# Attention output of a hybrid decoder step: queries on partitions, divided after the product, in place of probabilities scaled before it

## The chip, the cores and the metric

The kernel runs on one core of one Trainium2 chip. The metric is the device time of one execution in microseconds (us); three runs of the kernel before took 1811.17, 1813.03 and 1814.5 us, so its median is 1813.03 us. Besides these there is one profiled execution, from which all rows below come.

## The reference, cut to what matters

The program is one inference step of a two-layer decoder trunk for 512 prompt tokens and 64 sample tokens. Each layer projects its input, runs sparse attention and a gated linear recurrence (GLA) beside each other, merges both with gates, and ends in a SwiGLU block. The change is in the attention of the prompt tokens: 8 heads of 64, 4 key/value heads, and each query keeps its best 128 keys.

```python
logits = jnp.einsum('bqhgd,bqkhd->bqhgk', qg, k_sel) * HEAD_DIM ** -0.5
logits = jnp.where(valid[:, :, None, None, :], logits, -jnp.inf)
p = jax.nn.softmax(logits, axis=-1)
o = jnp.einsum('bqhgk,bqkhd->bqhgd', p, v_sel)
...
merged = sigmoid(gate_a) * (attn_o @ w_oa) + sigmoid(gate_b) * (g_out @ w_ob)
```

The kernel computes logits against all keys up to the query and masks those that are not kept, so that nothing is gathered.

## The kernel before, in words

All activations stand turned, features on partitions and the 576 tokens along the free axis, in two halves of 288. Weights are read panel by panel; a panel is 128 output features. Each is split into a high and a low part (w_hi by ScalarE in line 1996, w_lo by GpSimd in line 1895), and a panel is worked off in eight parts of six matmuls (line 1460): high by high, high by low, low by high, each for two halves.

The class Plan writes out one list of steps; every engine walks through this list and issues what is its own, so the order on each engine's queue is the list's order. Where smaller work lies beside the panels, the method woven spreads the parts of the panels over a list of items: each item has a weight (FILL, 1.0 where it names none), and after an item come as many parts as its weight's share of all the parts. The stretch of the change holds the last 80 parts of the gate panels (gr, gta, gtb) against the items of the GLA's norm, the sample group's attention, and then the prompt's attention.

The prompt's attention goes through four blocks j of 128 queries, and in each through 8 heads h; block j has j+1 blocks of 128 keys. Head number n = 8j+h takes this way. PE computes its logits (lines 1475 and 1476) while head n-2 is handled. The vector engine masks them in place and takes the maximum (max_head, line 2408). ScalarE writes the exponentials to p_t, of which there are two, and their sum to p_sum (line 2005). The vector engine takes the reciprocal of the sum and multiplies p_t by it (scale_head, lines 2417 and 2419); in the queue of the vector engine the scaling of head n+1 stands ahead of the maximum of head n+2. PE turns p_t block by block by transposes into PSUM bank 2 (line 1859), and ScalarE copies that to pT_t (line 2335). After every second head the step attn_pv multiplies for both heads of one key/value head (line 1871): V's 128x64 slice is the stationary operand, the turned probabilities of 128 queries stream, and the result has features on partitions, the even head on the lower 64 and the odd head on the upper. The four products of a block fill PSUM bank 3, the use ("o", j). After the last one the step attn_t has ScalarE copy the bank to attn_t (line 2342).

Behind the stretch stands the step mix: ScalarE splits gla_o and then attn_t into in_hi (lines 2264 and 2269), the vector engine makes in_lo (line 2373), and PE starts the output panels (oab). It can start once the last gtb panel is done, because in_hi is the input of the gtb panels up to then. SP loads the first weights of the SwiGLU block when ("o", 3) is ready.

Other names in the rows: soT (line 1845) turns the sample group's output, four PE instructions with 128x128 weights and 64 streamed columns; k_t,qz (line 1811) are logits of the sample group; gate_b (line 2462) is the vector engine's eviction of a gate panel out of PSUM; q_split and k_hi (line 2323) are ScalarE's splits of the next block's queries and keys.

Of the kernel before, what the change touches and what calls it, by code (L numbers as in the profile page):

```python
# [17 lines left out]
F32 = mybir.dt.float32  # L18
# [9 lines left out]
P = 128  # L28
# [14 lines left out]
HD = 64  # L43
# [40 lines left out]

FILL = {"intra": 2.0, "intra_out": 1.5, "kv": 1.0, "sround": 2.0, "attn": 1.0, "attn_pv": 0.4, "attn_t": 0.2,
        "topk": 0.5, "kcT": 1.0, "slog": 2.4, "gnorm": 2.0}
# [158 lines left out]
class Plan:  # L245
# [220 lines left out]
    def build_layer(self, base):  # L466
# [81 lines left out]
        for j, h in order:  # L548
            items.append([("attn", j, h)])
            if h < 5 and j < 3:  # L550
                items[-1] += [("qk", j + 1, i) for i in ((0, 1), (2,), (3,), (4,), (5,))[h]]
            if h % 2:
                items.append([("attn_pv", j, h // 2)])
            if h == N_HEADS - 1:
                items[-1].append(("attn_t", j))
        self.woven(range(split, first["oab"]), items)
# [59 lines left out]
    def extra_step(self, step):  # L616
# [61 lines left out]
        if kind == "attn_pv" and step[2] == 0:  # L678
            self.open(("o", step[1]), 3)
        if kind == "gnorm":  # L680
            self.open(("gn", step[1], 0), 0)
            self.open(("gn", step[1], 1), 1)
            self.stage(("gn", step[1]), "bank_ready", ("gn", step[1], 1))
            self.gate_tmp(("gn", step[1]), "gnorm_done", self.layer * GH + step[1] + 1)
# [3 lines left out]
def build(nc, A):  # L688
# [4 lines left out]
    with ctx:  # L693
# [124 lines left out]
        pT_t = sub("pT_t", [P, 2, 4, P])  # L818
        o_pairs = at("o_pairs", [P, 2, KV_W], F32, off[0])
        sub("o_pairs_kept", [P, ATTN_W])  # L820
        cursor[0] = max(off[0], end1, ar + 2 * turned + 2 * FF_SLOTS * 4 * P * 4)
# [107 lines left out]
        pv_done = semaphore("pv_done")  # L929
        p_scaled = semaphore("p_scaled")  # L930
        p_inverted = semaphore("p_inverted")
# [429 lines left out]
        def _(e):  # L1361
# [24 lines left out]
            def body():  # L1386
# [133 lines left out]
                for layer, step in plan.steps:  # L1520
# [329 lines left out]
                    elif kind == "attn":  # L1850
                        _, j, h = step
                        n = j * N_HEADS + h
                        if n == 0:
                            logits(0)
                            logits(1)
                        e.wait_ge(p_scaled, nth(n + 1, len(ORDER)))
                        e.wait_ge(free(("pT", j, h)), opened(("pT", j, h)))
# [5 lines left out]
                    elif kind == "attn_pv":  # L1863
                        _, j, kv = step
                        if kv == 0:
                            e.wait_ge(free(("o", j)), opened(("o", j)))
                        for u in range(2):
                            e.wait_ge(free(("pT", j, 2 * kv + u)), emptied(("pT", j, 2 * kv + u)))
                        for s in range(j + 1):
                            for u in range(2):  # L1870
                                ins = e.matmul(aux[64 * u:64 * u + 64, 3, kv * P:(kv + 1) * P],  # L1871
                                               kv_rows[:, s, KV_W + kv * HD:KV_W + (kv + 1) * HD], pT_t[:, u, s, :],
                                               start=(s == 0), stop=(s == j), skip_group_check=True)
                        if kv < N_KV - 1:
                            ins.then_inc(pv_done, 1)
                        else:
                            ins.then_inc(ready(("o", j)), 1)

            body()
# [90 lines left out]
        def _(e):  # L1970
# [18 lines left out]
            def body():  # L1989
# [30 lines left out]
                for layer, step in plan.steps:  # L2020
# [237 lines left out]
                    elif kind == "mix":  # L2258
# [6 lines left out]
                        else:  # L2265
                            e.wait_ge(free(("so",)), emptied(("so",)))
                            e.wait_ge(free(("o", 3)), emptied(("o", 3)))
                            for kt in range(4, KD):
# [70 lines left out]
                    elif kind == "attn_t":  # L2339
                        j = step[1]  # L2340
                        e.wait_ge(ready(("o", j)), filled(("o", j)))
                        e.activation(attn_t[:, :, j * P:(j + 1) * P], aux[:, 3, :].rearrange("p (m n) -> p m n", m=4),
                                     ACT.Copy).then_inc(free(("o", j)), 1)

# [4 lines left out]
        def _(e):  # L2349
# [18 lines left out]
            def body():  # L2368
# [31 lines left out]
                def max_head(n):  # L2400
# [9 lines left out]
                    e.wait_ge(max_done, turn(max_done))  # L2410

                def scale_head(n):

                    j, h = ORDER[n]
                    key = ("log", j, h)
                    e.wait_ge(free(key), emptied(key))
                    e.reciprocal(p_inv[:, h:h + 1], p_sum[:, j % 2, h:h + 1]).then_inc(dve_step, 1)
                    e.wait_ge(dve_step, turn(dve_step))
                    e.tensor_scalar(p_t[:, n % 2, 0:(j + 1) * P], p_t[:, n % 2, 0:(j + 1) * P], p_inv[:, h:h + 1], None,
                                    ALU.mult).then_inc(p_scaled, 1)  # L2420

                for layer, step in plan.steps:
# [473 lines left out]
                    elif kind == "spT":  # L2896
                        i = step[1]
                        if i >= 2:
# [6 lines left out]
                                      aux[0:NS, 2, 2 * P:3 * P]).then_inc(free(("spT", i)), 1)  # L2905
                        e.wait_ge(free(("spT", i)), emptied(("spT", i)))
                    elif kind == "attn":
                        _, j, h = step
                        n = j * N_HEADS + h
                        L = (j + 1) * P  # L2910
                        if n == 0:
                            max_head(0)
                            max_head(1)
                            scale_head(0)
                        if n + 1 < len(ORDER):
                            scale_head(n + 1)
                        if n + 2 < len(ORDER):
# [35 lines left out]
```

## Time and profile before

| what | value |
|---|---|
| runs | 1811.17, 1813.03, 1814.5 us (median 1813.03) |
| profiled execution | 1812.7 us, of which the span is 1810.9 us |
| mean granted TensorE clock | 0.992 |
| busy | PE 1743.2 us (96%), PE weight load 1634.2 (90%), vector engine 1092.6 (60%), ScalarE 795.9 (44%), GpSimd 784.1 (43%) |
| DMA | 151.06 MB, mean 83 GB/s |

The span goes from the first to the last instruction; the 1.8 us around it belong to the execution's time. PE's busy time is the time in which a matmul is under way; matmuls are pipelined, so records overlap and a busy PE need not be at its peak. The chain of waits is followed back from the last instruction, at each step to what released it. In a timeline a row stands for one or several instructions of one kind in a row: start, length from the first start to the last end, engine, line, operands, count, and in brackets how long the engine idled before and what ended that.

### The profile page before, as it was taken

To read this page: it belongs to the slowest core of one execution; us is meant where nothing else is said; L and a number is where in the kernel's file an instruction comes from. 1 tells how busy PE (TensorE), PEld (TensorE's weight loads), DVE (VectorE), ACT (ScalarE), POOL (GpSimd) and SP (SyncE) were. 2 spreads that over 40 slices of the span, in tenths; PEclk is the share of its full clock that TensorE was granted. 3 is DMA by queue.
4 is the path that set the end of the run, shared out by engine and by line. 5 is a ranking of instruction groups with operands and counts; after the bars stand their busy time and mean duration, and the time that the engine had idled before them with its cause. 6 is when DMAs were issued, how large, how long until landed. Compare 5 with 4: busy or idle time off the path is not lost.

```text
span 1810.9 us, 33288 instructions
## 1 busy us (share of the span) xinstructions
PE 1743.2 (96%) x12738; PEld 1634.2 (90%) x12738; DVE 1092.6 (60%) x2142; ACT 795.9 (44%) x1539; POOL 784.1 (43%) x510
## 2 busy tenths in 40 slices
PE   8999999999999999999999899999999999999998
PEld 6885898789999999999988768987899999999998
DVE  3856776455587437537537567845647873574463
ACT  4442214564466336426434322236645662463352
POOL 2323451533446447446333323525234563563452
PEclk9999999999999999999999999999999999999999
DMA  4232234214323423413222222351233233234122
GB/s 156 69 86 70 61 89 124 59 36 129 93 59 94 119 68 94 116 43 88 62 74 74 62 74 74 80 143 40 78 94 105 56 97 109 67 94 114 50 57 79
DMA packets 263303, 151.06 MB, mean 83 GB/s; under 512 B 15910, under 2 KB 255594, under 8 KB 263146
## 3 DMA queue, kind: packets, MB, share of 16 engines
q1 hardware_dynamic: 263146, 148.94, 29.3%
q8 instruction: 102, 1.67, 0.4%
q14 instruction: 55, 0.45, 0.1%
HBM read 141.53 MB, written 7.37 MB: 82 GB/s over the span
## 4 chain that ended last, share of the span: by engine, by line
PE 79%; DVE 13%; ACT 4%; issue 3%; DMA 1%; SPq 0%; POOL 0%; DVEq 0%; ACTq 0%; POOLq 0%
PE prod L1460 36%; PE prod L1514 8%; PE prod L1515 8%; PE prod L1516 8%; PE prod L1404 2%; PE prod L1405 2%; PE prod L1406 2%; PE aux L1871 1%; PE aux L1859 1%; DVE in_lo L2373 1%; PE aux L1834 1%; DVE aux L2619 1%; DVE scores L2788 1%; PE aux L1632 1%; ACT w_hi L1996 1%
## 5 line engine op out<-in xcount | busy, mean ns | idle before, releaser
L1895 POOL TENSOR_TENSOR w_lo<-w_raw,w_hi 128x1024 fp32r<-128x1024 f32 (+2 forms) x160 | 370.3, 2314 | 735.2 <-ACT w_hi L1996 730.7
L1996 ACT ACTIVATE w_hi<-w_raw 128x1024 fp32r<-128x1024 f32 (+2 forms) x160 | 163.0, 1019 | 269.4 <-PE prod L1460 236.3
L1460 PE MATMUL prod<-in_hi,w_hi 128*128 128x288 f32 x1024 | 236.7, 313 | 10.2 <-DVE in_lo L2373 7.8
L1460 PE MATMUL prod<-in_hi,w_lo 128*128 128x288 f32 x1024 | 223.0, 300 | 0.0
L1460 PE MATMUL prod<-in_lo,w_hi 128*128 128x288 f32 x1024 | 222.7, 300 | 0.0
L1514 PE MATMUL prod<-t_hi,ff_hi 128*128 128x288 f32 x704 | 208.6, 296 | 1.2 <-ACT in_sum L2050 0.6
L1460 PE MATMUL prod<-mid_hi,w_hi 128*128 128x288 f32 x960 | 207.6, 298 | 2.1 <-DVE mid_lo L2373 2.1
L1515 PE MATMUL prod<-t_lo,ff_hi 128*128 128x288 f32 x704 | 207.9, 295 | 0.0
L1516 PE MATMUL prod<-t_hi,ff_lo 128*128 128x288 f32 x704 | 207.1, 294 | 0.0
L1460 PE MATMUL prod<-mid_lo,w_hi 128*128 128x288 f32 x960 | 206.3, 296 | 0.0
L1460 PE MATMUL prod<-mid_hi,w_lo 128*128 128x288 f32 x960 | 206.3, 296 | 0.0
L1460 PEld LDWEIGHTS prod<-in_hi,w_hi 128*128 128x128 f32 x1024 | 167.5, 193 | 27.2 <-issue 19.1
L1460 PEld LDWEIGHTS prod<-in_hi,w_lo 128*128 128x128 f32 x1024 | 168.5, 193 | 0.0
L1460 PEld LDWEIGHTS prod<-in_lo,w_hi 128*128 128x128 f32 x1024 | 168.1, 193 | 0.0
L1907 POOL TENSOR_TENSOR ff_lo<-ff_sum,ff_hi 128x512 fp32r<-128x512 f32 x88 | 126.9, 1445 | 81.7 <-ACT ff_hi L2046 81.3
L1460 PEld LDWEIGHTS prod<-mid_hi,w_hi 128*128 128x128 f32 x960 | 153.6, 188 | 3.5 <-DVE mid_lo L2373 3.5
L1514 PE MATMUL prod<-in_hi,ff_hi 128*128 128x288 f32 x528 | 156.3, 296 | 0.4 <-issue 0.4
L1515 PE MATMUL prod<-in_lo,ff_hi 128*128 128x288 f32 x528 | 155.8, 295 | 0.0
L1516 PE MATMUL prod<-in_hi,ff_lo 128*128 128x288 f32 x528 | 155.6, 295 | 0.0
L1460 PEld LDWEIGHTS prod<-mid_hi,w_lo 128*128 128x128 f32 x960 | 154.0, 188 | 0.0
L1460 PEld LDWEIGHTS prod<-mid_lo,w_hi 128*128 128x128 f32 x960 | 153.9, 188 | 0.0
L1514 PEld LDWEIGHTS prod<-t_hi,ff_hi 128*128 128x128 f32 x704 | 132.1, 188 | 2.9 <-issue 1.8
(332 smaller groups left out, 3688.1 us busy)
## 6 DMA issues: line engine op xcount, KB each, us to landing
w_raw<-in_w_in SPq DMA_DIRECT2D x72, 512.0 KB, 3.7
ff_gate<-in_w_ffn_gu SPq DMA_DIRECT2D x44, 512.0 KB, 5.0
ff_up<-in_w_ffn_gu SPq DMA_DIRECT2D x44, 512.0 KB, 3.9
w_raw<-in_w_ffn_down SPq DMA_DIRECT2D x32, 512.0 KB, 3.8
w_raw<-in_w_o SPq DMA_DIRECT2D x16, 512.0 KB, 3.7
w_raw<-in_w_ffn_down SPq DMA_DIRECT2D x16, 384.0 KB, 3.3
k_pages<-in_cache_k SPq DMA_DIRECT2D x32, 128.0 KB, 2.1
v_pages<-in_cache_v SPq DMA_DIRECT2D x32, 128.0 KB, 2.1
```

The lines of the kernel that those rows point to most:

```text
L1404: e.matmul(out, in_hi[:, kt, tok], hi_w, start=first, stop=False)
L1405: e.matmul(out, in_hi[:, kt, tok], lo_w, start=False, stop=False)
L1406: ins = e.matmul(out, in_lo[:, kt, tok], hi_w, start=False, stop=last)
L1460: ins = e.matmul(slot(g)[:, h, :], w[:, slot_w, i * P:(i + 1) * P], a[:, i, h * HALF:(h + 1) * HALF], start=first, stop=last)
L1514: e.matmul(out, ff_hi[:, q % FF_SLOTS, w], hi, start=first, stop=False, skip_group_check=True)
L1515: e.matmul(out, ff_hi[:, q % FF_SLOTS, w], lo, start=False, stop=False, skip_group_check=True)
L1516: ins = e.matmul(out, ff_lo[:, q % FF_SLOTS, w], hi, start=False, stop=(k == 3), skip_group_check=True)
L1632: ins = e.matmul(aux[:, bank(key), 0:L], qi_t[rows, h // 2, j * P:(j + 1) * P], ki_t[rows, 0:L], start=True, stop=True)
L1834: ins = e.matmul(aux[64 * u:64 * u + 64, bank(("spo", i)), 0:KV_W], pT_t[0:n, i % 2, s, 64 * u:64 * u + 64], v, start=(s == 0), stop=(s == 2),
L1895: e.tensor_tensor(w_lo[:, p % 2, 0:n], w_raw[:, p % RAW_RING, 0:n], w_hi[:, p % 2, 0:n].bitcast(F32), ALU.subtract).then_inc(w_lo_done, 1)
L1907: e.tensor_tensor(ff_lo[:, q % FF_SLOTS, :], ff_weights(name, b), ff_hi[:, q % FF_SLOTS, :].bitcast(F32), ALU.subtract).then_inc(ff_lo_don ...
L1996: e.activation(w_hi[:, p % 2, 0:n], w_raw[:, p % RAW_RING, 0:n], ACT.Copy).then_inc(w_hi_done, 1)
```

## The change

The exponentials are no longer scaled. The transposes of a head wait for its exponential itself. In attn_pv the operands change places: the turned exponentials of 128 queries are the stationary operand (128x128) and a 128x64 slice of V streams, so the result has queries on partitions and the 8 heads' 64 features each along the free axis of bank 3. A new step attn_norm on the vector engine takes the reciprocals of the block's eight sums at once and multiplies the bank by them into o_rows. A new step attn_t on PE turns o_rows by four transposes back into bank 3, a use of its own, ("ot", j), and ScalarE copies that as before. The weaving gets items for these: attn_norm with weight 0.2 after the last product of a block, the turning with the next block's first head, and at the end an empty item and the turning of block 3, each at 1.0.

```diff
-FILL = {... "attn_pv": 0.4, "attn_t": 0.2,
+FILL = {... "attn_pv": 0.4, "attn_norm": 0.2,
...
                 items.append([("attn_pv", j, h // 2)])
+            if h == 0 and j:
+                items[-1].append(("attn_t", j - 1))
             if h == N_HEADS - 1:
-                items[-1].append(("attn_t", j))
+                items.append([("attn_norm", j)])
+        items += [[], [("attn_t", 3)]]
...
+        if kind == "attn_t":
+            self.open(("ot", step[1]), 3)
...
+        o_rows = at("o_rows", [P, N_HEADS, HD], F32, off[0])
...
# PE, attn
-                        e.wait_ge(p_scaled, nth(n + 1, len(ORDER)))
+                        e.wait_ge(free(("log", j, h)), emptied(("log", j, h)))
...
# PE, attn_pv
-                        for s in range(j + 1):
-                            for u in range(2):
-                                ins = e.matmul(aux[64 * u:64 * u + 64, 3, kv * P:(kv + 1) * P],
-                                               kv_rows[:, s, KV_W + kv * HD:KV_W + (kv + 1) * HD], pT_t[:, u, s, :],
+                        for u in range(2):
+                            for s in range(j + 1):
+                                h = 2 * kv + u
+                                ins = e.matmul(aux[:, 3, h * HD:(h + 1) * HD], pT_t[:, u, s, :],
+                                               kv_rows[:, s, KV_W + kv * HD:KV_W + (kv + 1) * HD],
                                                start=(s == 0), stop=(s == j), skip_group_check=True)
...
+                    elif kind == "attn_t":
+                        j = step[1]
+                        e.wait_ge(free(("o", j)), emptied(("o", j)))
+                        for m in range(4):
+                            ins = e.transpose(aux[:, 3, m * P:(m + 1) * P],
+                                              o_rows[:, 2 * m:2 * m + 2, :].rearrange("p h d -> p (h d)"), ident)
+                        ins.then_inc(ready(("ot", j)), 1)
...
# ScalarE, mix and attn_t
-                            e.wait_ge(free(("o", 3)), emptied(("o", 3)))
+                            e.wait_ge(free(("ot", 3)), emptied(("ot", 3)))
...
-                        e.wait_ge(ready(("o", j)), filled(("o", j)))
+                        e.wait_ge(ready(("ot", j)), filled(("ot", j)))
...
# vector engine
-                def scale_head(n):
-
-                    j, h = ORDER[n]
-                    key = ("log", j, h)
-                    e.wait_ge(free(key), emptied(key))
-                    e.reciprocal(p_inv[:, h:h + 1], p_sum[:, j % 2, h:h + 1]).then_inc(dve_step, 1)
-                    e.wait_ge(dve_step, turn(dve_step))
-                    e.tensor_scalar(p_t[:, n % 2, 0:(j + 1) * P], p_t[:, n % 2, 0:(j + 1) * P], p_inv[:, h:h + 1], None,
-                                    ALU.mult).then_inc(p_scaled, 1)
...
+                    elif kind == "attn_norm":
+                        j = step[1]
+                        e.wait_ge(free(("log", j, N_HEADS - 1)), emptied(("log", j, N_HEADS - 1)))
+                        e.reciprocal(p_inv[:], p_sum[:, j % 2, :]).then_inc(sums_inverted, 1)
+                        e.wait_ge(sums_inverted, nth(j + 1, 4))
+                        e.wait_ge(ready(("o", j)), filled(("o", j)))
+                        e.tensor_tensor(o_rows[:], aux[:, 3, :].rearrange("p (h d) -> p h d", d=HD),
+                                        bcast(p_inv[:], 2, HD), ALU.mult).then_inc(free(("o", j)), 1)
+                        e.wait_ge(free(("o", j)), emptied(("o", j)))
...
-                            scale_head(0)
-                        if n + 1 < len(ORDER):
-                            scale_head(n + 1)
```

## Rows read from the trace of the kernel before

**Rows 1.** The page, part 4: the chain that ended last, by engine.

```profile
PE 79%; DVE 13%; ACT 4%; issue 3%; DMA 1%; SPq 0%; POOL 0%; DVEq 0%; ACTq 0%; POOLq 0%
```

**Rows 2.** Windows: length, busy time (instructions) by engine, clock, DMA share, GB/s.

```profile
331.24:411.02 79.78, 72.54 (x582) 65.19 (x581) 44.07 (x136) 49.01 (x131) 31.10 (x25) 0.98 0.13 37
...
334.70:338.10 3.40, 3.40 (x17) 3.38 (x16) 1.82 (x8) 2.32 (x8) 2.00 (x2) 0.50 0.54 154
1229.00:1232.40 3.40, 3.40 (x17) 3.38 (x15) 1.25 (x6) 2.13 (x8) 2.38 (x3) 0.50 0.51 148
```

**Rows 3.** Waits of PE, whole span: us in total, times, longest.

```profile
PE prod L1460 <- DVE in_lo L2373: 7.8, 4, 2.2
...
PE aux L1871 <- ACT pT_t L2335: 5.3, 10, 1.2
...
PE aux L1859 <- DVE p_t L2419: 3.9, 4, 1.8
```

**Rows 4.** Timeline of PE, a product of block 0 and one of block 3.

```profile
350.16 0.43 PE L1460 MATMUL prod<-in_hi,w_lo 128*128 128x288 f32 x2
350.53 0.44 PE L1871 MATMUL aux<-pT_t,kv_rows 128*64 128x128 f32 x4
350.89 0.53 PE L1460 MATMUL prod<-in_hi,w_hi 128*128 128x288 f32 x2
...
397.44 0.43 PE L1460 MATMUL prod<-in_hi,w_lo 128*128 128x288 f32 x2
397.80 1.09 PE L1871 MATMUL aux<-pT_t,kv_rows 128*64 128x128 f32 x16
398.83 0.66 PE L1859 MATMUL aux<-cst,p_t 128*128 128x128 f32 x4
```

**Rows 5.** Timeline of PE, a head of block 3.

```profile
396.02 0.60 PE L1859 MATMUL aux<-cst,p_t 128*128 128x128 f32 x4
396.37 0.47 PE L1475 MATMUL aux<-k_hi,q_split 128*128 128x512 f32 x1
...
396.91 0.43 PE L1460 MATMUL prod<-in_hi,w_hi 128*128 128x288 f32 x2
```

**Rows 6.** Timeline of PE around soT.

```profile
329.74 0.42 PE L1460 MATMUL prod<-in_hi,w_lo 128*128 128x288 f32 x2
330.00 0.55 PE L1845 MATMUL aux<-cst,o_pairs 128*128 128x64 f32 x4
330.37 0.51 PE L1460 MATMUL prod<-in_hi,w_hi 128*128 128x288 f32 x2
```

**Rows 7.** Timeline of PE, logits of the sample group.

```profile
300.28 0.40 PE L1811 MATMUL aux<-k_t,qz 128*64 128x64 f32 x8
```

**Rows 8.** Groups by line, vector engine: busy, mean ns; idle before, releaser.

```profile
L2462 DVE TENSOR_TENSOR gate_b<-prod,rstd 128x576 f32<-128x576 f32 x16 | 12.1, 758 | 12.9 <-PE prod L1460 12.6
```

**Rows 9.** Timelines of ScalarE and PE at the first head.

```profile
332.72 0.19 ACT L2005 ACTIVATION_READ_ACCUMULATOR p_t<-aux,neg_max 128x1 f32 x1
...
333.98 0.33 PE L1859 MATMUL aux<-cst,p_t 128*128 128x128 f32 x1 [1.78 <-DVE p_t L2419]
```

**Rows 10.** Timeline of ScalarE at the start of block 1.

```profile
351.70 0.59 ACT L2342 ACTIVATE attn_t<-aux 128x512 f32<-128x512 f32 x1
...
353.43 0.62 ACT L2323 ACTIVATE q_split<-q_t 64x512 fp32r<-64x512 f32 x1
...
354.26 0.36 ACT L2335 ACTIVATE pT_t<-aux 128x256 f32<-128x256 f32 x1
```

**Rows 11.** Groups by line, PE's weight loads: busy, mean ns; idle before, releasers.

```profile
L1859 PEld LDWEIGHTS aux<-cst,p_t 128*128 128x128 f32 x160 | 19.3, 140 | 8.4 <-DVE p_t L2419 4.7 <-issue 3.8
L1871 PEld LDWEIGHTS aux<-pT_t,kv_rows 128*64 128x64 f32 x320 | 17.3, 136 | 11.6 <-ACT pT_t L2335 7.9 <-issue 3.7
```

**Rows 12.** Timelines of ScalarE and PE at the stretch's end.

```profile
409.41 2.39 ACT L2264 ACTIVATE in_hi<-gla_o 128x576 fp32r<-128x576 f32 x4
...
411.02 0.50 PE L1460 MATMUL prod<-in_hi,w_hi 128*128 128x288 f32 x2 [2.15 <-DVE in_lo L2373]
```

More of the change, by code:

```diff
@@ L83 @@
 Y_STORES = {3: 0, 6: 4, 7: 7}
-FILL = {"intra": 2.0, "intra_out": 1.5, "kv": 1.0, "sround": 2.0, "attn": 1.0, "attn_pv": 0.4, "attn_t": 0.2,
+FILL = {"intra": 2.0, "intra_out": 1.5, "kv": 1.0, "sround": 2.0, "attn": 1.0, "attn_pv": 0.4, "attn_norm": 0.2,
         "topk": 0.5, "kcT": 1.0, "slog": 2.4, "gnorm": 2.0}
@@ L929, in build @@
         pv_done = semaphore("pv_done")
-        p_scaled = semaphore("p_scaled")
+        sums_inverted = semaphore("sums_inverted")
         p_inverted = semaphore("p_inverted")
@@ L2340, in body @@
                         j = step[1]
-                        e.wait_ge(ready(("o", j)), filled(("o", j)))
+                        e.wait_ge(ready(("ot", j)), filled(("ot", j)))
                         e.activation(attn_t[:, :, j * P:(j + 1) * P], aux[:, 3, :].rearrange("p (m n) -> p m n", m=4),
-                                     ACT.Copy).then_inc(free(("o", j)), 1)
+                                     ACT.Copy).then_inc(free(("ot", j)), 1)
             body()
```

## The prediction

> **What bounds the kernel now.** I read the page's chain of waits first: TensorE (PE) is 79% of what ended last and the vector engine 13% [rows 1], so a change pays only where it alters PE's own instructions or a wait of PE. The view by windows narrows it to the stretch that the change touches: 79.78 us in the first layer, PE busy in 72.54, mean granted clock 0.98; behind the 0.98 stands one piece of 3.4 us at 0.50, which is 1.2 of 2.4 GHz, and a like piece in the second layer [rows 2]. The table of PE's waits names what stands in that stretch over both layers: 5.3 us for pT_t, 3.9 us for the scaled p_t, and half of the 7.8 us for in_lo, at the stretch's end [rows 3]. Last comes the timeline of PE, for the price of each group of instructions.
>
> I count per layer; both run the same plan. A panel's part is three pairs of matmuls; a pair begins 0.265 us after the one before (it is 0.43 long, and the next overlaps it). A group's price is the gap before it beyond that step, its run to the next start, and what the instruction behind it is longer than usual.
>
> **The second product (attn_pv).** The number of matmuls stays: 8(j+1) in block j, two PE instructions each, so 16 groups per layer of 4, 8, 12 or 16 instructions, four of each. Now 64 columns of V are the weights and 128 columns stream. A group of 4: from 350.16+0.265 to 350.53 a gap of 0.10, 0.36 to the next start, and the pair behind is 0.53 long for 0.43: 0.56 us. A group of 16: gap 0.095, 1.03 to the next start, and the transposes behind are 0.66 long where other fours are 0.60: 1.19 us [rows 4, 5]. In a line between them: 0.56, 0.77, 0.98, 1.19; four of each are 14.0 us.
> Afterwards the weights are 128 columns (a turned block of exponentials) and 64 stream. One group of before has that shape in both operands, soT: its four instructions begin without a gap, take 0.37 to the next start, and the pair behind is 0.51 long for 0.43: 0.45 us, 0.11 an instruction [rows 6]. In proportion: 0.44, 0.88, 1.32, 1.76; four of each are 17.6 us. So **+3.6 us**: short groups get cheaper, long ones dearer. Bounds: without what follows the group, 0.37/4 = 0.093 a step, 2.7 us less; on the other side transposes of 0.60/4 = 0.15, their first one's start included, 6 us more. Further off lies k_t,qz (64 columns as weights, 64 streamed): eight in 0.40, 0.05 each at most [rows 7]; by it the groups come to 8 us, 6 less than before. I stay with soT, which is alike in both operands.
> The Trainium skill (TensorE: Matmul & The Clock Gate, section Back-to-back issue gap) gives streamed columns / 2.4 GHz + 2.5 ns for a back-to-back matmul, 29 ns here; by it the groups would come to some 5 us. soT speaks against it for full weights, and the same section warns that weight load and matmul both set the pace.
>
> **The new transposes (attn_t on PE).** Four 128x128 transposes per block, 16 per layer. A group of four takes 0.35 to the next start [rows 5]; with 0.08 behind it, as after soT, 0.43: **+1.7 us** (bounds 1.4 and, at its full length of 0.60, 2.4).
> The Trainium skill (TensorE: Matmul & The Clock Gate, Part 4: PE-mode transpose) gives about 275 ns for a transpose within a kernel. Four in a row cost 0.35 in the trace; by the page's figure the sum would be some 2.7 us more per layer.
>
> **The division (attn_norm).** Per block one reciprocal of 128x8 and one product of 128x512 out of PSUM; the nearest row is gate_b, 0.76 at 576 columns [rows 8], so 0.7, and about 0.95 with drain and signals from the last product's end to the first turning transpose (bounds 0.7 and 1.3). What lies beside it follows from the weaving: the items' weights rise from 67.0 to 69.8 (four norms of 0.2, an empty item and attn_t at 1.0), the parts per unit fall from 80/67 = 1.194 to 1.146. A head's transposes and logits take 0.89 for four key blocks, so 0.22 a block [rows 5]; a part takes 3 x 0.265 = 0.8. Rounded out, behind block 0's last product come a part and a head of two blocks (1.24), covered; behind block 1's only a head of three (0.67), short by 0.3; behind block 2's a head of four, short by 0.1; behind block 3's two parts, covered. **+0.4 us.** Behind the waiting product on the vector engine stands the next block's third maximum, whose logits PE issues about when the product ends: nothing.
>
> **The removed scaling.** 32 reciprocals and 32 products per layer leave the vector engine, which is not the bound. PE sees:
> (a) the start. The first exponential's sum is out at 332.72+0.19 = 332.91, PE starts at 333.98 after 1.78 idle [rows 9]; released by ScalarE it starts about 0.1 behind the sum: **-0.96**.
> (b) the clock. Right behind that gap PE runs 3.4 us at 0.50, in both layers [rows 2]. With a gap of about 0.9 I expect full speed, worth half the piece: **-1.7** (bounds 0 and -1.7).
> (c) one further wait for a scaling, 3.9/2-1.78: **-0.2** [rows 3].
> (d) the waits for pT_t, 2.65. The loop of exponential, reciprocal, scaling, next maximum, next exponential is cut, since no maximum stands behind a scaling any more. Not all goes: at block 1's first product ScalarE works off q_split to pT_t from 353.43 to 354.62, and the copy attn_t (0.59), which stood ahead of that head's exponentials, moves in between [rows 10]. I count 0.6 of wait there and 1.1 in small ones elsewhere: **-0.95** (bounds +0.5, where two more copies show, and -2.65).
> (e) gaps ahead of weight loads that the profile puts down to issue, 3.8 and 3.7 in both layers [rows 11]; most of that lies under a matmul still running. I give **-0.5** (0 to -1.9).
>
> **The end of the stretch.** The last parts of gtb now follow the turning, and the split of gla_o starts only behind them. Before, PE idled 2.15 after the last product; from the split's start to PE's next matmul are 411.02-409.41 = 1.61 [rows 12], with a signal 1.7: **-0.4** (0 to -0.5). Block 3's copy is hidden under the last part; if it were not, it costs its 0.6. SP's loads of ff_gate still wait for the last product, and the weights' steps on ScalarE and POOL keep their panels: nothing.
>
> **Sum** per layer: 3.6+1.7+0.4-0.96-1.7-0.2-0.95-0.5-0.4 = +1.0; two layers **+2.0 us**. The profiled execution has a span of 1810.9 and a time of 1812.7, so it would take 1814.7; it lies 0.3 below the median of the runs, 1813.0, to which +2.0 gives **1815.0**.
>
> **Rivals.**
> 1. The clock still falls (slower). One mechanism at one place: PE's gap at the first head, then about 0.9 us and among short transposes and logits, still brings 0.50 behind it. Price 2 x 1.7: 1818.4. For it: it fell in both layers. Against: the 0.98 over the whole stretch leaves room for one such piece only, so none followed the 1.2 us wait for pT_t [rows 2, 3]. It decides from one layer on: 1816.7 with one.
> 2. All waits go (faster). With the loop cut, (d) and (e) empty to their bounds: 2 x (1.7+1.4) = 6.2 more, 1808.8. For it: each maximum stood behind an exponential. Against: ScalarE's own queue, with the copy moved into it.
> 3. Streamed columns set the product's price (the rule above): at 0.05 a step 2 x 9.6 less, 1795.8. Only k_t,qz speaks for it, and its weights are half as wide.
> 4. The turning does not fit its cover (slower): the o bank is held by product, division, turning and copy, and a block's first product waits for the copy. If that costs 0.7, a copy and its signal, at three blocks of both layers: +4.2, 1819.2. ScalarE has 49 of 79.78 us to do [rows 2], so I think it rare.
>
> **How the numbers follow.** Forecast 0.47; rival 1 0.2, rival 4 0.1, rival 2 0.19, rival 3 0.04. About 0.2% (3.6 us) is what a measurement of this kernel tells from no change, so 1809.4 to 1816.6 is the same. The forecast's own spread is some +-4 (the product's step, (d)), which lends a little to both sides: faster 0.25, same 0.43, slower 0.32. Range 1807.5 to 1820.5: from a little below rival 2 to a little above rivals 1 and 4; left out are rival 3 and cases in which two costs add.
>
> **What would show it.** The product's group of 16 takes about 1.76 us and begins without a gap, the group of 4 gets shorter. The turning transposes take 0.35 and wait at most 0.3 for o_rows. PE's gap before the first transposes is near 0.9, and the window behind it shows clock 1.00. The waits for pT_t fall from 5.3 to some 3.5, the largest at block 1's first product. The gap before the output panels is near 1.7. I am wrong if the product's step is not near 0.11, if the clock stays at 0.50 there, or if PE waits more for pT_t than before.

## The result: slower, 1832.2 us for the 1815.0 predicted

The changed kernel took 1832.2 us (median of 4 runs, 1827.5 to 1835.8), the kernel before 1813.0 beside it: ratio 1.0104, 95% interval [1.0083, 1.0125]. Timed once more among the experiments, it took 1825.5 us (6 runs) beside 1814.1, ratio 1.0074 [1.0056, 1.0092]. So it is slower by 19 us in the one and by 11 us in the other; the prediction had +2.0 and a range that ended at +7.5. What differs between the two timings is in part 6 of the experiments.

Its chain of waits reads as before, TensorE (PE) first [rows 1]:

```profile
PE 80%; DVE 12%; ACT 4%; issue 2%; DMA 1%; SPq 0%; POOL 0%; DVEq 0%; ACTq 0%; POOLq 0%
```

The stretch of [rows 2], from the sample group's last product to the output panels, and the two pieces right behind the first head (columns: length, busy us and instructions of PE, PEld, DVE, ACT, POOL, granted clock, DMA share, GB/s):

```profile
335.58:421.73 86.15, 80.29 (x604) 76.49 (x603) 26.57 (x80) 50.76 (x132) 30.76 (x25) 0.98 0.15 42
338.10:341.50 3.40, 3.40 (x17) 3.38 (x17) 0.72 (x4) 2.27 (x9) 3.07 (x3) 0.51 0.12 15
1239.30:1242.70 3.40, 3.40 (x16) 3.38 (x16) 0.72 (x4) 2.43 (x9) 3.18 (x3) 0.50 0.18 32
```

The vector engine has lost 17.5 of its 44.1 us. PE is busy 7.8 us longer, of which 0.8 is a part that the new weaving moved into the stretch. Behind the first head the clock is still at 0.50 in both layers.

PE's waits over the whole span (total us, times, longest), to be laid beside [rows 3]:

```profile
PE prod L1466 <- DVE in_lo L2387: 6.8, 4, 1.7
PE aux L1878 <- ACT pT_t L2349: 4.5, 10, 0.7
...
PE aux L1865 <- ACT p_t L2019: 2.8, 2, 1.4
```

So 1.0, 0.8 and 1.1 us of waiting have gone, over both layers. The rest of the answer is in PE's own instructions. Timelines of PE: a product of block 3, to be laid beside [rows 4], then block 0's turning and the stretch's end, beside [rows 12]:

```profile
397.57 0.43 PE L1466 MATMUL prod<-in_hi,w_lo 128*128 128x288 f32 x2
397.84 1.89 PE L1878 MATMUL aux<-kv_rows,pT_t 128*128 128x64 f32 x16
399.57 0.60 PE L1865 MATMUL aux<-cst,p_t 128*128 128x128 f32 x4
...
353.47 0.60 PE L1889 MATMUL aux<-cst,o_rows 128*128 128x128 f32 x4
353.83 0.52 PE L1466 MATMUL prod<-in_hi,w_hi 128*128 128x288 f32 x2
...
421.73 0.50 PE L1466 MATMUL prod<-in_hi,w_hi 128*128 128x288 f32 x2 [1.68 <-DVE in_lo L2387]
```

The group of 16 begins one step (0.27) behind the pair ahead of it, without a gap, and takes 1.73 to the next start, where it took 1.03. This turning takes 0.36 and waits for nothing.

**Where the start's gain went.** Timelines of ScalarE, the vector engine, POOL and PE at the first head, layer 1:

```profile
334.93 1.35 ACT L2319 ACTIVATE attn_t<-aux 64x64 f32<-64x64 f32 x8 [1.62 <-PE aux L1851]
336.30 1.06 ACT L2010 ACTIVATE w_hi<-w_raw 128x1024 fp32r<-128x1024 f32 x1
337.38 0.37 ACT L2019 ACTIVATE p_t<-aux,neg_max 128x128 f32<-128x128 f32 x1
...
336.54 0.14 DVE L2422 DVE_READ_ACCUMULATOR2_ANT neg_max<- 128x1 f32 x1
...
337.89 0.33 PE L1865 MATMUL aux<-cst,p_t 128*128 128x128 f32 x1 [1.38 <-ACT p_t L2019]
```

The masked maximum is ready at 336.68, but ScalarE starts the exponential at 337.38: a panel's w_hi stands ahead of it. Before, that panel's start lay one item earlier (w_hi at 329.66). The items' new weights moved it, as they move every part.

### The profile page after: what moved, and what is told of

It is laid out like the page before. It is cut to its first block, busy times and chain, and to the rows that moved or that the text cites. A ratio compares the mean times of both kernels' runs of the same rounds, so it can differ in the third digit from the quotient of the medians.

```text
span 1830.2 us, 33256 instructions
## 1 busy us (share of the span) xinstructions
PE 1762.6 (96%) x12770; PEld 1659.8 (91%) x12770; DVE 1058.6 (58%) x2030; ACT 798.1 (44%) x1539; POOL 784.0 (43%) x510
## 4 chain that ended last, share of the span: by engine, by line
PE 80%; DVE 12%; ACT 4%; issue 2%; DMA 1%; SPq 0%; POOL 0%; DVEq 0%; ACTq 0%; POOLq 0%
PE prod L1466 36%; PE prod L1520 8%; PE prod L1521 8%; PE prod L1522 8%; PE prod L1410 2%; PE aux L1878 2%; PE prod L1411 2%; PE prod L1412 2%; PE aux L1865 1%; PE aux L1840 1%; DVE aux L2623 1%; DVE scores L2792 1%; PE aux L1638 1%; DMA x_rows<-in_x_prompt 1%; DVE mid_lo L2387 1%
```

## The experiments

Times are medians; a ratio is to the kernel before on the same chip. "At full clock" means a length less half of what of it lay at 0.50. The attention region is that of the last 80 input parts ahead of the output panels of a layer.

**1. The scaling alone (e1), the product alone (e2), the weaving alone (e3), and the change without its weaving (e4).**

e1 takes the scaling out of the kernel before and puts nothing in its place:

```
-                            scale_head(0)
-                        if n + 1 < len(ORDER):
-                            scale_head(n + 1)
```

> The kernel before with the scaling of the exponentials left out (its attention output is therefore not divided by the sums); products, weaving and layouts as before. Theory 1 (the price of the product's instructions and of the turning makes the loss, and the removed scaling gives little): the first transposes start about 1 us earlier per layer, one wait of 0.2 goes, the waits for pT_t shrink by less than half; 1 to 4 us less than before, 1809 to 1812; more only if the halved clock behind the first head goes (3.4 less). Rival (the freed vector engine is worth much, and the changed product takes it back): 6 us less or more.

Measured: 1809.6 us, ratio 0.9979 [0.9967, 0.9991]. Theory 1 holds: some 4 us are all that the removed scaling is worth. The start's gap is 0.78 in both layers, and no clock of 0.50 stands behind it.

e2 exchanges the operands of the second product and copies the result unturned; the probabilities are still scaled:

```
-  e.matmul(aux[64 * u:64 * u + 64, 3, kv * P:(kv + 1) * P], kv_rows[..], pT_t[:, u, s, :],
+  e.matmul(aux[:, 3, h * HD:(h + 1) * HD], pT_t[:, u, s, :], kv_rows[..],
```

> The kernel before, still scaled and woven as before, with the operands of the second product exchanged as in the change and nothing else: the result stands with queries on partitions and is copied unturned, so the output is in the wrong places. Theory 1: the 160 PE instructions per layer step by 0.11 in place of 0.055, less what short groups save at their entry and exit; 4 to 5 us per layer, +8 to +10 us, 1821 to 1823. Theory 2 (the loss is clock and weaving, the product costs as predicted): at most +7. Rival 3 of the prediction (streamed columns): less than before.

Measured: 1820.8 us, 1.0051 [1.0031, 1.0071]. At full clock the attention region of a layer is 5.0 us longer, as theory 1 has it; the time, 7.1 us more, lies at the border of the two theories.

e3 gives the kernel before the changed kernel's items and weights, with pauses where it has its new steps:

```
-        "attn_t": 0.2,
+        "pause": 0.2,
+                items.append([("pause",)])
+        items += [[], []]
```

> The kernel before with the weaving weights of the changed one (a pause of 0.2 after each block, two empty items at the end) and nothing else. Theory 1: the halved pieces of the clock outside the attention come and go by themselves, and a panel's w_hi ahead of the first exponential costs 0.5 us per layer: within 2 us of before. Theory 2 (the halved pieces ahead of and behind the attention come from the other weaving): 4 to 8 us more than before, and the granted clock falls to 0.50 in the stretches of the gate panels in which it fell in the changed kernel.

Measured: 1818.2 us, 1.0030 [1.0018, 1.0041]. Theory 1 missed: in the kernel with the scaling, the weaving costs some 4.5 us by itself. Theory 2 had the size, but not the place: there are 6.8 us at 0.50 around the first head in both layers, twice as much as before. At full clock the two regions are only 0.1 and 0.9 us longer than before, so most of the 4.5 us is clock. The timelines of e3 show why (ScalarE, vector engine, POOL, PE):

```profile
336.00 1.06 ACT L1998 ACTIVATE w_hi<-w_raw 128x1024 fp32r<-128x1024 f32 x1
...
337.84 1.77 DVE L2421 TENSOR_SCALAR p_t<-p_t,p_inv 128x128 f32<-128x128 f32 x1
...
337.19 2.34 POOL L1897 TENSOR_TENSOR w_lo<-w_raw,w_hi 128x1024 fp32r<-128x1024 f32 x1 [1.73 <-issue]
...
339.67 0.48 PE L1861 MATMUL aux<-cst,p_t 128*128 128x128 f32 x1 [3.43 <-DVE p_t L2421]
```

w_hi delays the exponential, and its w_lo then lies beside the first scaling, which takes 1.77 us; PE waits 3.43.

e4 is the changed kernel with item weights that put every part up to block 3's last heads where it was before:

```
-  "attn_norm": 0.2,
+  "attn_norm": 0.0,   # and 0.4, 0.4, 0.2, 0.8, 0.6 for the last items
```

> The changed kernel with the parts spread as before up to the last pair of heads of block 3 (the division weighs nothing, and the last items share the old weights). Theory 1: 1 to 2 us less than the changed kernel, since the first exponential no longer stands behind a w_hi; about 1830. Theory 2: 5 to 8 us less, about 1825, with as many halved pieces of the clock as before.

Measured: 1823.3 us, 1.0058 [1.0038, 1.0077], 9 us less than the first timing of the changed kernel and more than either theory gave; timed beside the changed kernel (part 6) it is 1821.8 for 1825.5. The gap is 0.78, and no 0.50 stands in the attention of either layer.

**2. The w_hi by itself (f1).** The changed kernel, with the panel's `weights` step added behind the first head where its start falls right ahead of it:

```
+  late = n < len(items) and items[n][:1] == [("attn", 0, 0)]   # self.weights(p + 1) follows that item
```

> The changed kernel with one step moved in both layers: the panel's w_hi (1.06 us on ScalarE) that its weaving put ahead of the first two exponentials goes behind them (its w_lo on POOL one step later with it). Theory 1 (that w_hi is what kept the start's gap): TensorE's gap ahead of the first head's transposition falls from 1.38 us to 0.8 us, as in the two kernels where no w_hi stood there; the 3.4 us at granted clock 0.50 right behind it go; 2 x (0.6 + 1.7) = 4.6 us less than the changed kernel's 1832, so about 1827.5 (1825 to 1829.5). Theory 2 (the loss from the weaving is spread over where parts and pauses fall, not at this place): within 2 us of the changed kernel, 1830 to 1834.

Measured: 1825.0 us, 1.0067 [1.0054, 1.0080], 7 us less than the first timing of the changed kernel. PE at the first head:

```profile
338.09 0.33 PE L1874 MATMUL aux<-cst,p_t 128*128 128x128 f32 x1 [0.78 <-ACT p_t L2028]
```

Theory 1 holds for the gap, 0.78 as predicted, and no 0.50 follows. The time is less clear: the waits for pT_t grew by 1.1 us a layer, and at full clock the region is no shorter (139.2 for 138.2 in layer 1). Against the second timing of the changed kernel, 1825.5, nothing is left.

**3. The attention's start ahead of the first head (f2).** The kernel before, with a step of its own for the first two logits, maxima, exponentials and the first scaling, and three parts behind it:

```
+        items.append([("attn_start",)])     # FILL "attn_start": 2.4
```

> The kernel before, its scaling and its product kept, with the start of the attention as a step of its own: the first two heads' logits, masked maxima and exponentials and the first scaling are issued one step ahead of the first head, with three parts of the product between (weight 2.4). Theory 1 (the start's gap and the clock behind it are all that the unscaled start could ever gain): 1.78 us idle and 1.7 us of halved clock go in each layer, 2 x 3.5 = 7 us less than before, about 1806.7 (1804 to 1809.5). Theory 2 (the parts that fill the gap are missing later, in front of other waits): the idle time comes back within the attention, within 2 us of before.

Measured: 1816.4 us, 1.0021 [1.0011, 1.0031]. Theory 1 missed. The gap only fell to 1.07, because the first scaling took 1.80 us beside w_lo (0.71 before). Two runs asked whether that was the cause.

> The run with the start as a step of its own (weight 2.4, w_lo beside the start), without the scaling: the output is left undivided. Theory 1 (the vector engine's scaling is what waits for POOL's w_lo, its masked maximum and ScalarE's exponential do not): no gap ahead of the first transposition, masked maxima at 0.30 us beside w_lo; some 2 us less than the run without scaling, about 1806 to 1809. Theory 2 (the start is late for another reason): the gap stays near 1 us.

Measured (f2 without the scaling, output undivided): 1808.7 us, 0.9978 [0.9962, 0.9994], no gap, and a masked maximum of 128 columns keeps its 0.30 us beside w_lo. Theory 1 holds.

g1 moves the panel start away from the scaling (`"slog": 2.8`):

> The kernel before with the attention's start as a step of its own, as in the run before, but with the sample logits' weight at 2.8 for 2.4, so that the panel start (w_hi on ScalarE, w_lo on POOL) falls one item earlier and neither stands beside the first scaling. Theory 1 (in the run before the first scaling took 1.80 us for 0.29 because POOL's w_lo ran until 0.09 us before its end; without that neighbour the start is covered): the first scaling takes at most 0.7 us, TensorE's gap ahead of the first transposition goes from 1.07 to under 0.2 us, no halved clock behind it; 2 x (1.8 + 1.7) less than before where nothing comes back, and 1806 to 1811 as parts are missing further on. Theory 2 (the idle time returns at the waits for pT_t): within 2 us of before.

Measured: 1824.9 us, 1.0055 [1.0031, 1.0078]. The start did what theory 1 said, gap 0.00, and yet the run is 11 us slower. The idle time came back at the waits for pT_t, where theory 2 put it, and more of it than theory 2 allowed (within 2 us of before). In 330 to 420 us PE waits 5.8 us for pT_t ahead of the product (columns: instructions, busy us, mean ns, idle before and its releaser), where it waited 2.6:

```profile
L1872 PE MATMUL aux<-pT_t,kv_rows 128*64 128x128 f32 x160 | 12.3, 281 | 6.1 <-ACT pT_t L2336 5.8
```

**4. Does the scaling wait for POOL (h1)?** In the trace of before 13 of the 64 scalings are lengthened, by 9.8 us together; each has an instruction of POOL beside it that was running when it began, and ends 0.08 to 0.29 us behind that one's end. h1 writes a sum that nothing reads:

```
-                                    ALU.mult).then_inc(p_scaled, 1)
+                                    ALU.mult, ALU.add, accum_out=p_seen[:, h:h + 1]).then_inc(p_scaled, 1)
```

> The kernel before with one edit: the scaling of the exponentials also writes the sum of what it wrote (accum_out), a value that nothing reads. The Trainium skill (SBUF - State Buffer, section Who interferes with whom) says that tensor_scalar shares a port pair with GpSimd except in the form that writes its accumulator. Theory 1 (the scaling waits for POOL at a shared port): no scaling is longer than 0.9 us beside an instruction of POOL, where 13 of 64 were lengthened by 9.7 us together in the trace of before; the start's gap falls from 1.78 to about 1.5 us, and the time is 0 to 4 us less than before. Theory 2 (the scaling waits for its operand): the same heads stay lengthened, to 1.8 and 1.9 us, and the time is 0 to 5 us more, for the further instruction of 0.14 us a head that reads the accumulator.

The same head (block 0, head 7) before and in h1, vector engine and POOL:

```profile
347.36 1.79 DVE L2419 TENSOR_SCALAR p_t<-p_t,p_inv 128x128 f32<-128x128 f32 x1
...
346.68 2.39 POOL L1895 TENSOR_TENSOR w_lo<-w_raw,w_hi 128x1024 fp32r<-128x1024 f32 x1 [0.36 <-POOL k_lo L1919]
```

```profile
346.13 0.35 DVE L2420 TENSOR_SCALAR_CACHE_REDUCE p_t<-p_t,p_inv 128x128 f32<-128x128 f32 x1
...
345.45 2.38 POOL L1896 TENSOR_TENSOR w_lo<-w_raw,w_hi 128x1024 fp32r<-128x1024 f32 x1 [0.36 <-POOL k_lo L1920]
```

w_lo begins 0.68 us ahead of the scaling in both. Before, the scaling ends with it; in h1 it takes 0.35 us as all eight of its size do. Theory 1 holds, and the start's gap is 1.43. The time does not follow: 1813.2 us, 0.9997 [0.9988, 1.0005]. The run trades the 9.8 us of lengthening for a longer form (0.35 to 0.75 us for 0.29 to 0.49, 10.2 us in all) and a read of the sum (0.08 us each), on an engine that is not the bound, and the time shows neither. What the lengthening by itself cost on the path is not separated by this run; at the start it was 0.35 us a layer (1.78 to 1.43).

i1 and i2 are f2 and g1 with this scaling:

> The kernel before with the start as a step of its own (weight 2.4) and the scaling in the form that also writes its sum. Theory 1 (in the run with that start alone, the first scaling waited for POOL's w_lo, 1.80 us for 0.29): the first scaling takes 0.35 us, the gap ahead of the first transposition goes from 1.07 us to under 0.2, and the time falls from 1816 to about 1807 to 1811, 3 to 7 us under before. Theory 2 (the order of the parts costs what the start wins): 1814 to 1818, not faster than before.

> The run that took 1825 us (start as a step of its own, sample logits' weight 2.8), with the scaling in the form that also writes its sum. Theory 1 (its waits for pT_t, 5.9 us in a layer, come from 8 scalings a layer that POOL lengthens): these waits fall to about 3 us, and the time to 1811 to 1817. Theory 2 (they come from where its parts fall): they stay above 5 us, and the time above 1821.

Measured: i1 1811.9 us, 0.9986 [0.9971, 1.0001]; i2 1822.9 us, 1.0050 [1.0033, 1.0067]. For i1 theory 1 holds in the gap, 0.00; the time is 4.5 us less than f2's and lies 0.9 above theory 1's range, and whether it is faster than the kernel before stays open. For i2 theory 2 holds: 5.8 us of waits for pT_t in a layer without any lengthened scaling. They come from where the parts fall, since i2 differs from i1 by the one weight.

**5. What the turning costs (f3) and what sets the product's price (f4).** Both start from e4. f3 keeps one of four transposes:

```
-                        for m in range(4):
+                        for m in range(1):
```

> The changed kernel with the weaving of before up to block 3's last heads (1823.3 us), and one of the four transposes of each block's turning kept: three quarters of the attention output are left unturned. Theory 1 (the turning costs its 16 slots of 0.096 us in a layer, in line on TensorE): 2 x 12 x 0.096 = 2.3 us less, about 1821 (1819.5 to 1822). Theory 2 (the turnings stand where TensorE would wait for pT_t in any case): within 1 us of 1823.3.

Measured: 1823.1 us, 1.0059 [1.0043, 1.0074], the same as e4. Groups of PE in one layer's 64 parts, e4 and then f3:

```profile
L1885 PE MATMUL aux<-kv_rows,pT_t 128*128 128x64 f32 x160 | 20.4, 275 | 3.9 <-ACT pT_t L2356 3.8
L1896 PE MATMUL aux<-cst,o_rows 128*128 128x128 f32 x16 | 2.5, 279 | 0.2 <-DVE o_rows L2924 0.2
```

```profile
L1885 PE MATMUL aux<-kv_rows,pT_t 128*128 128x64 f32 x160 | 20.4, 275 | 4.9 <-ACT pT_t L2356 4.7
L1896 PE MATMUL aux<-cst,o_rows 128*128 128x128 f32 x4 | 1.2, 301 | 0.2 <-DVE o_rows L2924 0.2
```

Twelve slots (1.3 us) have gone and 1.0 us of waiting for pT_t has come: PE gets to the next product sooner and finds pT_t not copied. Theory 2 is the nearer one.

f4 streams 128 columns in each matmul of the product:

```
-  e.matmul(aux[:, 3, h * HD:(h + 1) * HD], pT_t[:, u, s, :], kv_rows[:, s, KV_W + kv * HD:KV_W + (kv + 1) * HD],
+  e.matmul(aux[:, 3, kv * P:(kv + 1) * P], pT_t[:, u, s, :], kv_rows[:, s, c:c + P],
```

> The same kernel (1823.3 us), with 128 columns streamed in each of the 160 matmuls of the product instead of 64 (both heads of a pair then land in the same columns, so half of the output is another head's). Theory 1 (an f32 matmul of this shape costs its 128-column weights, not its streamed columns): the slot stays at 0.109 us, within 2 us of 1823.3. Theory 2 (streamed columns set the price): the slot doubles to about 0.22 us, 2 x 160 x 0.109 = 35 us more, about 1858.

Measured: 1825.8 us, 1.0077 [1.0064, 1.0090]; starts within a group are 0.111 to 0.112 us apart, as with 64 columns. A group of block 3:

```profile
396.98 2.02 PE L1885 MATMUL aux<-kv_rows,pT_t 128*128 128x128 f32 x16
398.84 0.60 PE L1872 MATMUL aux<-cst,p_t 128*128 128x128 f32 x4
```

Theory 1 holds for the step; the time is 2.5 us above e4's where theory 1 allowed 2 and theory 2 asked for 35. The prediction's rival 3 falls with theory 2. The formula behind it stands in the Trainium skill (TensorE: Matmul & The Clock Gate, section Back-to-back issue gap) for a matmul by itself, with the warning that it counts too little where few columns stream. The step of 0.111 us agrees with that warning and not with the formula's 29 ns.

**6. What comes and goes.** The two kernels unchanged, for second profiles, and then the changed kernel timed beside e4:

> The kernel before once more, for a second profile. Theory 1 (a stretch of halved clock follows from the order of work at its place): the pieces at 0.50 stand at the same places, behind the first head in both layers above all. Theory 2 (they come by chance): behind the first head they are missing in a layer or both.

> The changed kernel once more, for a second profile. Theory 1: the piece at 0.50 behind the first head is there in both layers, and those at 208, 266 and 297 us too. Theory 2: those ahead of the attention, where nothing was changed, stand elsewhere or not at all, and only the sum of them is like.

> The changed kernel, timed once more. Theory 1 (product, turning and weaving cost some 13 us of work at full clock, and the rest of the first comparison was stretches of halved clock that come and go): 1825 to 1830, ratio 1.006 to 1.009. Theory 2 (the whole loss belongs to the change): again 1832, ratio 1.0104.

> The changed kernel with the weaving of before up to block 3's last heads, timed beside the changed kernel on one chip. Theory 1 (the new weaving costs the start's gap of 0.6 us and halved clock behind it in both layers): 4 to 9 us less than the changed kernel of this call. Theory 2 (the difference of the first call was the chip's): within 2 us of it.

Measured: one execution each of 1819.3 and 1825.2 us; then 1825.5 us, 1.0074 [1.0056, 1.0092] for the changed kernel, as theory 1 has it, and 1821.8, 1.0048 [1.0036, 1.0060] for e4, 3.7 less, between its two theories. Behind the first head both second profiles have the piece at 0.50 again, in both layers; of those at 208, 266 and 297 us in the changed kernel only the first is there again. The pieces outside the attention differ from profile to profile of the same kernel: together, whole span, they and the others make 28.8 and 37.9 us in the two profiles of before, and 41.3, 32.0 and 27.3 us in the three of the changed kernel. Half of such a sum is time where PE is busy throughout, so 7 us of the 1832 in the first profile of the changed kernel against its third are of this kind.

At full clock the spans are 1796.5 and 1798.5 before, 1809.5, 1807.4 and 1809.4 after, and 1805.3 and 1807.1 in e4. Two profiles are few for a difference of some us: what lies outside the two attention regions takes 1527 to 1535 us at full clock in the 19 profiles, whichever the kernel. Two other readings are steadier. A region at full clock takes 131.8 to 132.2 us in the profiles of before, 138.2 to 138.8 in those of the changed kernel and 138.8 to 138.9 in e4's, so the change costs 12.5 to 14 us over both layers. And each run's span times its mean granted clock is its length at full clock: on average (the clock is on record to three places, 0.9 us either way for a single run) 1794.6 us in the 95 runs of the kernel before that were timed beside the experiments, 1809.5 and 1809.2 us in the two timings of the changed kernel. So **13 to 15 us of work is what the change costs**, in both timings alike.

What differs between the timings is the clock: the first lost 20.6 us to it on average (span less length at full clock), the second 15.5, and the kernel before 17.1. Over all its runs the changed kernel lost 17.4 us, so nothing here shows that the change makes such pieces likelier. By the same reckoning e4 takes 1808.3 us at full clock and lost 13.1 us (12 runs), so its 3.7 us are clock, about the 3.4 us that the prediction's (b) gives for a start without the piece; as work, the new weaving costs about 1 us, which these few runs hardly tell from nothing.

## Why the prediction was wrong

The 64 parts of the input panels around the attention, one layer of before and one of the changed kernel's third profile, which has no 0.50 there (columns as above):

```profile
302.34:411.02 108.68, 101.35 (x810) 88.28 (x809) 50.48 (x151) 59.73 (x155) 41.15 (x32) 0.98 0.21 60
```

```profile
306.37:419.42 113.05, 106.94 (x826) 97.26 (x825) 33.00 (x95) 59.99 (x153) 40.89 (x32) 1.00 0.22 63
```

At full clock that is 107.0 and 113.05, so +6.1 us a layer, where the prediction's terms without the clock (b) make +2.7. The whole region of 80 parts:

```profile
277.36:411.02 133.66, 123.72 (x978) 108.11 (x977) 68.88 (x184) 73.59 (x180) 46.40 (x34) 0.99 0.26 74
```

```profile
280.62:419.42 138.80, 129.30 (x994) 117.09 (x993) 51.38 (x128) 74.37 (x180) 46.13 (x34) 1.00 0.27 76
```

At full clock these are 131.96 and 138.80, +6.8; the further 0.8 is a wait that the prediction did not look at (the last point of the list). The terms, each group's price taken from one start to the next less the waits:

- **The product with (e): +3.1 predicted, +5.8 measured. This is the step that failed most.** What it takes now was right: 0.11 a step, 17.5 us for 17.6. What it took before was not: 14.0 predicted, 11.2 in the trace. I had added a gap ahead of each group and a longer instruction behind it, 2.8 us in all, and let them go with the product. They belong to the change from one kind of matmul to another and mostly stayed: in e2 parts, transposes and logits together win 1.1 us. The gap of 0.09 ahead of a group did go where PE does not wait for pT_t (6 of 16 groups in the third profile), and the same 0.16 stands ahead of the others as before. The short groups did not get cheaper either: those of 4 take 0.36 to 0.47 to the next start less the wait, for 0.37. Inside the groups 144 steps went from 7.9 to 15.9 us, and the last steps of the 16 groups from 3.3 to 1.6. The product alone costs +6.3, its neighbours give back 0.5. The loads' "issue" waits of [rows 11] did fall, from 7.5 to 1.1 us over both layers (first profile), and brought PE no more than these 0.5.
- **The start, (a) and (c): -1.2 predicted, -0.7 measured.** The failed step is one sentence: that the weights' steps on ScalarE and POOL "keep their panels: nothing". The panel kept, but its w_hi came to stand ahead of the first exponential, and the gap became 1.38 where 0.82 was worked out. In e1, e4 and f1, where no w_hi stands there, it is 0.78.
- **The clock, (b): -1.7 predicted; in three profiles of the changed kernel 0.50 follows the first head in four of six layers.** The reasoning held and its condition failed. Over all profiles, behind a gap of 1.36 us or more the clock was at 0.50 within 2 us of its end in 11 of 16 layers; behind 1.15 or less in none of 22. Fourteen of these 22 had gaps of 0.78 to 1.15, so rival 1, that the clock falls behind a gap of about 0.9 as well, is not borne out; its effect came by the longer gap. Why the clock stayed up in the other five of the 16 is open.
- **The waits for pT_t, (d): -0.95 predicted, -0.2 measured** (2.8 to 2.6 before the products; the longest went from 1.2 to 0.7, and stands at block 3's third product, not at block 1's first, which waits 0.5). With the old weaving they even rise, to 3.8 in e4 and 3.3 in e1: PE is ready sooner, and the copies on ScalarE are not. That is also why rival 2 fell.
- **The turning: +1.7 predicted, +1.5 in slots**, of which f3 shows that most would have been waiting under the old weaving. The division: +0.4 predicted, +0.2 measured, all of it behind block 1's product; none behind block 2's. Rival 4 did not come: no product's wait ended with the bank.
- **The end: -0.4 predicted, -0.5 measured** (1.68 for 2.15).
- **Ahead of the prompt's attention: nothing predicted, +0.8 measured.** PE's gap ahead of the sample group's first logits (mask_s,repeat_b) is 1.9 us for 1.1 in every profile with the changed kernel's weights, and 1.1 in e4. The profile names no releaser; that the weaving moved it, the comparison with e4 shows. Before and third profile of the changed kernel, both layers:

```profile
PE aux L1801 <- issue: 2.2, 2, 1.1
```

```profile
PE aux L1807 <- issue: 3.7, 2, 1.9
```

A rule of the Trainium skill bears on what the scaling was: SBUF — State Buffer, section Who interferes with whom, says that VectorE and GpSimd share a pair of ports which one of them holds for its whole instruction, and that tensor_scalar can take it except in the form that writes its accumulator. The traces agree: 1.79 us beside w_lo, 0.35 in the form with a sum. It bears little on the price of the change, since h1 is as fast as before, but it is 1.5 us of e3's gap of 3.43 us.

## What to carry to other kernels

Price an exchange of operands by starts to starts of the same groups on both sides, look whether instructions of the group ran beside each other, and test whether the gaps around a group belong to it before letting them go with it. A new step in a list that shares out fill work by weight moves every later item: look what it puts ahead of the waits that you count on, on every engine. Taking work off an engine that is not the bound gains the few waits that stood on the path, here 4 us for 64 scalings, and it pays only if what replaces it on the bound engine is cheaper than that.

## What the hardware showed that was not expected

- With 128 columns of f32 weights the step in a group is 0.111 us, whether 64 or 128 columns are streamed (f4). The groups of before, with 64 columns of weights, make 0.055 a step ([rows 4]: 16 in 1.03, of which the last step takes 0.20). There two heads' instructions, one for each half of the output's partitions, begin 0.006 us apart, so that a pair takes 0.109. Narrow weights alone do not make it cheap. The trace of before has four transposes with 64 columns of weights and 128 streamed, all into the same half, and they begin 0.108 to 0.109 us apart:

```profile
161.21 0.60 PE L1651 MATMUL aux<-cst,kidx 128*64 128x128 f32 x4
```

  So what the exchange gave up is that two heads' products ran beside each other. No run shows this product itself with narrow weights and without its partner.
- A scaling from SBUF to SBUF waits for a running instruction of POOL (13 of 64 before, beside w_lo and k_lo): 0.29 us becomes up to 1.79. The masked maximum, which reads a PSUM bank, keeps its 0.30 beside the same w_lo.
- The same program shows 27 to 41 us at a granted clock of 0.50 from profile to profile, in pieces of 3.4 and 6.8 us but for the one that the span's end cuts.
